# The w2 loads of the expert stages move from the sync engine's queue to ScalarE's

## Chip, cores and metric

One core of one Trainium2 chip. The metric is the device time of one execution in microseconds (us); the median of the runs counts. All arithmetic is in 32-bit floats.

## What is computed

256 tokens of width 1024 pass through two layers of a first block and one of a second. Each of the three has a mixer (attention, and in two of them a gated linear recurrence beside it) and then a mixture of 32 experts. What bears on this case is the mixture:

```python
xr = xt[tok]
return (jax.nn.silu(xr @ w1[e]) * (xr @ w3[e])) @ w2[e]
```

w1 and w3 of an expert are 1024 x 512, w2 is 512 x 1024: 2 MB each (2,097,152 bytes), 6 MB for an expert, 32 experts in each of the three stages. Each token goes to two experts. The kernel reads the weights of every expert, whichever tokens it has. In the second block the three matrices are called w_gate, w_up and w_down.

## The kernel before, in words

The program runs mixer, experts, mixer, experts, mixer, experts. The expert stage is one function, `expert_stage` (from L151), built three times. It sorts the tokens by expert, so that each expert has a window of 32 seats in each of two tiles, and then runs one round over the 32 experts (further rounds run only if an expert has more tokens than seats).

**Buffers.** w1, w3 and w2 have three slots each (`Experts`, L75). Expert e uses slot e mod 3 for w3 and w2. The w1 of expert 3 goes to spare places in x and h, so that later w1 sit one slot lower and are asked for one expert earlier. The first three experts are asked for before the loop, in the mixer or in the stage's head.

**TensorE** (`tensor`, `step` at L427) does for expert e, in this order: `up_first(e)` (w1, L348), `turn(e-1)` (two transposes, L371), `up_second(e)` (w3, L348), `scatter(e-2)` (L406), `turn_sel` for every second expert (L395), `down(e-1)` (w2, L385). It says on semaphores what it has finished: `w1_used`, `up_done`, `down_done`. After expert 30's `up_second` the order is written out (L454 to L470): `down(29)`, `turn(30)`, two scatters, `turn_sel`, `down(30)`, `up_first(31)`, `up_second(31)`, scatter, `turn(31)`, `down(31)`, scatter. The last w3 and the last w2 are loaded in halves, each with its own semaphore (L118, L123).

**The sync engine (SP)** asks for all weights (`sync`, L218). In the loop its order for each step is: w3 of expert off once `up_done` says that the slot's last user is through, w2 of expert off-1 once `down_done` says so, w1 of expert off+1 once `w1_used` says so (`refill`, L248). At the end: w3(30), w2(29), w2(30), w1(31), w3(31) in halves, w2(31) in halves (L264 to L272). After the loop it asks for the next mixer's first three blocks, as `w1_used`, `up_done` and `down_done` reach their last values (L281 to L284).

**ScalarE** (`scalar`, L501) does for each expert `hidden(e)` (silu of the w1 product, L573), `window(u, e+2)` (two copies that cut the columns of expert e+2, L564), and in the third stage alone `result(e-1)`: it waits for `down_done` and copies half of the output (L479). In the first two stages VectorE takes the whole output with its gate (L482). VectorE does the rest: the product with w3's output, the copies of the transposes (L836, L839).

Of the kernel before, what the change touches and what calls it, by code (L numbers as in the profile page):

```python
# [16 lines left out]
E = 32  # L17
# [23 lines left out]
class Stage:  # L41
# [7 lines left out]
    def sem(self, name):  # L49
        self.sems.append(self.nc.alloc_semaphore(name=f"{self.name}_{name}"))  # L50
        return self.sems[-1]
# [99 lines left out]
def expert_stage(nc, stage, experts, x, h, hT, gate1, scale2, shift2, gate2, norm_w, consts, mem, ps, x_banks, turn_banks, following=None, store=None,  # L151
# [32 lines left out]
    down_done, dve_step = sem("down"), sem("dve_step")  # L184
# [23 lines left out]
    PAIRS = E // 2  # L208

    def steps(eng):  # L210

        return eng.value_load(nsteps[0:1, 0:1], min_val=1, max_val=ROUNDS)
# [5 lines left out]
    def sync(sp, loads=None):  # L218

        sp.wait_ge(out_made, 4)  # L220
        experts.load_up(sp, 2, 0, 1)
        sp.wait_ge(x_kept, 4)
        experts.load_down(sp, 2, 0, 1)
        sp.wait_ge(rows_ready, TILES)
        sp.wait_ge(placed, 1)
        experts.load_spare(sp, 0, x)
        sp.wait_ge(steps_ready, 1)
        sp.wait_ge(gathered, len(GATHERS))
        experts.load_spare(sp, 1, h)
        rounds = steps(sp)  # L230
        with sp.Fori(0, rounds) as r:
            def refill_w1(k, off):

                early = isinstance(k, int) and k == 0 and off <= experts.SPARE + 3
                sp.wait_ge(w1_used, r * E + k * 6 + (off - 3 if early else off - 2))
                experts.load_w1_of(sp, (off - 1) % 3, k * 6 + off)

            def refill_w3(k, off):

                sp.wait_ge(up_done, r * E + k * 6 + (off - 2))  # L240
                experts.load_w3_of(sp, off % 3, k * 6 + off)

            def refill_down(k, off):

                sp.wait_ge(down_done, r * E + k * 6 + (off - 2))
                experts.load_down_of(sp, off % 3, k * 6 + off)

            def refill(k, off):  # L248

                early = isinstance(k, int) and k == 0  # L250
                if early:
                    refill_w1(k, off + 1)
                refill_w3(k, off)
                if not early or off > 3:
                    refill_down(k, off - 1)
                if not early:
                    refill_w1(k, off + 1)

            for off in range(3, 6):
                refill(0, off)  # L260
            with sp.Fori(1, E // 6) as k:
                for off in range(6):
                    refill(k, off)
            last = E // 6  # L264
            refill_w3(last, 0)
            refill_down(last, -1)
            refill_down(last, 0)
            refill_w1(last, 1)
            sp.wait_ge(up_done, r * E + (E - 3))
            experts.load_last_w3(sp, 1)  # L270
            sp.wait_ge(down_done, r * E + (E - 3))
            experts.load_last_down(sp, 1)  # L272
            with sp.If(rounds > r + 1):

                sp.wait_ge(down_done, r * E + E)
                experts.load_spare(sp, 0, x)
                experts.load_spare(sp, 1, h)
                for slot, u, pair in ((0, 0, 0), (1, 1, 0), (2, 0, 1)):
                    experts.load_up(sp, slot, u, pair)
                    experts.load_down(sp, slot, u, pair)  # L280
        if following is not None:  # L281
            for n, freed in zip(range(following.AHEAD), (w1_used, up_done, down_done)):
                sp.wait_ge(freed, rounds * E)
                following.load(sp, n)  # L284
        if store is not None:
            sp.wait_ge(xw_ready, rounds * E + 1)
            loads(sp)
            for t in range(TILES):
                for c in range(2):
                    cols = slice(c * 512, (c + 1) * 512)  # L290
                    sp.wait_ge(end_ready, 2 * t + c + 1)
                    sp.dma_start(store[:, t, cols], h[:, t, cols]).then_inc(stored, 16)
            sp.wait_ge(stored, 16 * 2 * TILES)
# [183 lines left out]
    def copy_y(eng_copy, u, half):  # L477
        rows = slice(64 * half, 64 * half + 64)
        return eng_copy(y[rows, u, :], bank_Y[rows, :])  # L479
# [21 lines left out]
    def scalar(act):  # L501
# [58 lines left out]
        def window(u, at):  # L560

            for t in range(TILES):
                start = act.value_load(starts[0:1, t, bass.ds(at, 1)], min_val=0, max_val=PICKS)
                m = nc.scalar.copy(xw[:, u, :, t * SEATS:(t + 1) * SEATS], sorted_x[:, :, t, bass.ds(start, SEATS)])  # L564
            m.then_inc(xw_ready, 1)

        with act.Fori(0, rounds) as r:
            def hidden(e, u, first=False):

                act.wait_ge(up_done, e + 1)  # L570
                if not first:
                    act.wait_ge(hm_ready, e)
                nc.scalar.activation(sil, H1[u], ACT.Silu).then_inc(silu_done, 1)  # L573

            def result(e, u):

                if gate2 is None:
                    act.wait_ge(down_done, e + 1)
                    copy_y(nc.scalar.copy, u, 0).then_inc(y_copied[0], 1)

            window(1, r * E + 1)
            hidden(r * E, 0, True)
            hidden(r * E + 1, 1)
            result(r * E, 0)
            for u in range(2):
                window(u, r * E + (2 + u))
            with act.Fori(1, PAIRS - 1) as i:
                for u in range(2):
                    e = r * E + i * 2 + u
                    hidden(e, u)  # L590
                    window(u, e + 2)
                    result(e - 1, 1 - u)
            hidden(r * E + (E - 2), 0)
            result(r * E + (E - 3), 1)
            result(r * E + (E - 2), 0)
            hidden(r * E + (E - 1), 1)
            window(0, r * E + E)
            result(r * E + (E - 1), 1)
# [287 lines left out]
    def under_way(pool):  # L886
# [3 lines left out]
        for signal in (down_done, silu_done, hT_copied):  # L890
            pool.wait_ge(signal, 1)

    return sync, tensor, scalar, vector, out_made, under_way


# [3435 lines left out]
```

## Time and profile before

| | |
|---|---|
| median of 3 runs | 2014.52 us (2011.88 to 2015.36) |
| the profiled execution's own time | 2012.33 us |
| its span | 2010.6 us |
| TensorE busy | 1878.9 us (93%), mean granted clock 0.993 |
| ScalarE busy | 361.8 us (18%) |
| VectorE busy | 502.9 us (25%) |
| moved by DMA | 727.07 MB, mean 362 GB/s |
| DMA queue q1 | 725.26 MB |
| DMA queue q10 | 0.78 MB |

The span is the time from the first instruction to the last. The page cuts it into 40 slices of about 50 us; a "GB/s" figure stands for each. Engines are named PE (TensorE matmul), PEld (its weight load), DVE (VectorE), ACT (ScalarE), SP (the sync engine); a q behind a name (SPq, ACTq) marks what the engine's sequencer does, such as the issue of a DMA. A TensorE row says "busy" while the matmuls of a group run, whatever the pace at which their data came. All w1, w3 and w2 of the first two stages are called in_moe_w_dram in the rows; in the third they are in_w_gate_dram, in_w_up_dram and in_w_down_dram.

### The profile page before, as it was taken

The numbers are of one execution on the slowest core, as the hardware profiler recorded it, in microseconds if no ns is written. First come the engines' busy times: TensorE is split into PE (matmuls) and PEld (weight loads), VectorE is DVE, ScalarE is ACT, GpSimd is POOL, SyncE is SP. The second block draws the span as 40 slices with busy tenths as digits, with TensorE's granted clock in tenths as the row PEclk, the third lists the DMA queues.
The fourth block names the chain that finished last, engine by engine and source line by source line (L and its number), as shares of the span: only waits on it lengthen the run. The fifth ranks groups of instructions, "written<-read, shape, count | busy, mean of one in ns | idle before, by whom it ended". The sixth has DMA issues, their size and how long they took to land. (4 is left out here: it accounts for less than half of the span.)

```text
span 2010.6 us, 29251 instructions
## 1 busy us (share of the span) xinstructions
PE 1878.9 (93%) x11670; PEld 938.8 (47%) x11670; DVE 502.9 (25%) x1201; ACT 361.8 (18%) x804; POOL 3.1 (0%) x7
## 2 busy tenths in 40 slices
PE   6999999998888999999998888999999999998887
PEld 3444544444444345544444444455545544444443
DVE  1345311111111333511111111324544211111112
ACT  2332200000000232310000000224322111111111
POOL 0000000000000000000000000000000000000000
PEclk9999999999999899999999999999999999999999
DMA  9979999999999885899999999842238999999997
GB/s 355 313 264 349 423 426 426 427 428 428 428 428 416 297 288 197 355 427 426 427 428 428 428 428 427 284 156 96 85 126 342 419 426 427 427 428 428 428 428 304
DMA packets 117842, 727.07 MB, mean 362 GB/s; under 512 B 19471, under 2 KB 25978, under 8 KB 79754
## 3 DMA queue, kind: packets, MB, share of 16 engines
q1 hardware_dynamic: 116472, 725.26, 88.9%
q10 hardware_dynamic: 1298, 0.78, 0.2%
q8 instruction: 54, 0.88, 0.2%
q14 instruction: 18, 0.15, 0.0%
HBM read 724.17 MB, written 1.84 MB: 361 GB/s over the span
## 5 line engine op out<-in xcount | busy, mean ns | idle before, releaser
L348 PE MATMUL psum<-arena,norm_w 128*64 128x256 f32 x6048 | 722.4, 390 | 73.8 <-DMA arena<-in_moe_w_dram 46.7
L348 PEld LDWEIGHTS psum<-arena,norm_w 128*64 128x64 f32 x6048 | 419.9, 134 | 374.5 <-DMA arena<-in_moe_w_dram 68.2
L385 PE MATMUL psum<-arena,hT 128*64 128x512 f32 x1536 | 350.8, 598 | 6.4 <-DMA arena<-in_moe_w_dram 2.4
L573 ACT ACTIVATE hT<-psum 128x256 f32<-128x256 f32 x96 | 36.9, 384 | 994.8 <-PE psum L348 994.8
L385 PEld LDWEIGHTS psum<-arena,hT 128*64 128x64 f32 x1536 | 105.4, 136 | 210.3 <-issue 205.5
L2462 PE MATMUL psum<-arena,hT 128*128 128x512 f32 (+1 forms) x352 | 152.5, 582 | 0.4 <-DVE hT L2822 0.4
L482 DVE TENSOR_TENSOR hT<-psum,arena 128x512 f32<-128x512 f32 x64 | 44.3, 692 | 332.5 <-PE psum L385 332.5
L836 DVE COPY hT<-psum 128x256 f32<-128x256 f32 x96 | 40.8, 425 | 327.4 <-PE psum L371 327.4
L406 PE MATMUL psum<-hT 32*128 32x512 f32 x768 | 108.6, 638 | 2.4 <-DVE hT L482 1.6
L2462 PEld LDWEIGHTS psum<-arena,hT 128*128 128x128 f32 x352 | 64.3, 190 | 67.0 <-issue 63.9
L564 ACT COPY norm_w<-arena 128x256 f32 x192 | 78.7, 410 | 69.7 <-issue 69.5
L3817 PE MATMUL psum<-arena,hT 128*128 128x512 f32 x192 | 86.5, 605 | 0.9 <-DVE hT L4141 0.9
L839 DVE COPY hT<-psum 128x256 f32<-128x256 f32 x48 | 20.4, 425 | 231.2 <-PE psum L395 231.2
L3219 PE MATMUL psum<-arena,hT 128*128 128x512 f32 (+1 forms) x160 | 66.1, 568 | 1.6 <-PEq L1105 1.6
L479 DVE COPY hT<-psum 64x512 f32<-64x512 f32 x32 | 22.2, 695 | 166.1 <-PE psum L385 166.1
L3817 PEld LDWEIGHTS psum<-arena,hT 128*128 128x128 f32 x192 | 36.3, 194 | 46.3 <-issue 46.3
L371 PE MATMUL psum<-const_ident,hT 128*128 128x128 f32 x192 | 48.5, 334 | 3.5 <-DVE hT L834 3.5
L371 PEld LDWEIGHTS psum<-const_ident,hT 128*128 128x128 f32 x192 | 30.3, 207 | 44.8 <-issue 36.5
L406 PEld LDWEIGHTS psum<-hT 32*128 32x128 f32 x768 | 30.3, 183 | 42.0 <-issue 36.6
L757 DVE TENSOR_SCALAR arena<-const_iota,arena 128x64 f32<-128x64 f32 x204 | 49.7, 309 | 0.1
L834 DVE TENSOR_TENSOR hT<-hT,psum 128x256 f32<-128x256 f32 x96 | 39.8, 415 | 32.9 <-ACT hT L573 32.0
L3219 PEld LDWEIGHTS psum<-arena,hT 128*128 128x128 f32 x160 | 30.3, 193 | 32.6 <-issue 31.2
(438 smaller groups left out, 1200.4 us busy)
## 6 DMA issues: line engine op xcount, KB each, us to landing
arena<-in_moe_w_dram SPq DMA_DIRECT2D x186, 2048.0 KB, 32.3
arena<-in_w_gate_dram SPq DMA_DIRECT2D x31, 2048.0 KB, 30.1
arena<-in_w_up_dram SPq DMA_DIRECT2D x31, 2048.0 KB, 28.7
arena<-in_w_down_dram SPq DMA_DIRECT2D x31, 2048.0 KB, 30.5
arena<-in_ada_w_dram SPq DMA_DIRECT2D x24, 2048.0 KB, 15.3
arena<-in_w_in_dram SPq DMA_DIRECT2D x10, 2048.0 KB, 8.5
arena<-in_odd_w_in_dram SPq DMA_DIRECT2D x6, 2048.0 KB, 10.8
arena<-in_even_w_in_dram SPq DMA_DIRECT2D x4, 2048.0 KB, 18.9
```

The lines of the kernel that those rows point to most:

```text
L348: m = nc.tensor.matmul(out[64 * half:64 * half + 64, :].rearrange("p (q c) -> p q c", c=2), xw[:, u, c, :], w[c].rearrange("p (q half c) - ...
L371: m = nc.tensor.transpose(HT[:, c, :], hm[:, c::2], ident[:, :])
L385: m = nc.tensor.matmul(bank_Y[64 * half:64 * half + 64, :], hTs[:, k % 2, (k // 2) * 64:(k // 2) * 64 + 64], experts.slots[slot][2][:, k, ...
L406: nc.tensor.matmul(bank_acc[2 * t + half][:, :], selT[rows, u, :], y[rows, u, :], start=False, stop=False, skip_group_check=True).then_inc ...
L482: return nc.vector.tensor_tensor(y[:, u, :], bank_Y, gate2[:, 0:512], ALU.mult)
L564: m = nc.scalar.copy(xw[:, u, :, t * SEATS:(t + 1) * SEATS], sorted_x[:, :, t, bass.ds(start, SEATS)])
L757: m = nc.vector.tensor_scalar(at, iota[:, 0:SEATS].unsqueeze(1).to_broadcast([P, 2, SEATS]), slots[:, t, bass.ds(g, 1)], comb[:, t, bass.d ...
L834: nc.vector.tensor_tensor(hm, sil, H3[u], ALU.mult).then_inc(hm_ready, 1)
L836: nc.vector.tensor_copy(hTs, HT).then_inc(hT_copied, 1)
L2462: m = nc.tensor.matmul(banks[t][:, 0:width], hT[:, k, t * P:(t + 1) * P], ring.tile(n, DC, width)[:, k, :], start=(k == 0), stop=(k == DC ...
L3219: m = nc.tensor.matmul(side_bank("P", n, t)[:, 0:width], hT[:, k, t * P:(t + 1) * P], blocks.tile(("P", n))[:, k, :], start=(k == 0), stop ...
L3817: m = nc.tensor.matmul(side_bank("P", n, t), hT[:, c, t * P:(t + 1) * P], ring.tile(n, DC, 512)[:, c, :], start=(c == 0), stop=(c == DC - 1))
```

## The change

The three w2 requests of the sync engine's loop are taken out. ScalarE makes them, with the same semaphore and the same value to wait for, behind `hidden`, `window` and `result` of the same step. Its loop over pairs of experts becomes one over groups of six, since the slot (e mod 3) and the column buffer (e mod 2) have to be constants in the text. The first three w2 are still asked for by SP, and so are all further rounds' first three.

```diff
@@ sync
-            def refill_down(k, off):
-
-                sp.wait_ge(down_done, r * E + k * 6 + (off - 2))
-                experts.load_down_of(sp, off % 3, k * 6 + off)
-
             def refill(k, off):
                 early = isinstance(k, int) and k == 0
                 if early:
                     refill_w1(k, off + 1)
                 refill_w3(k, off)
-                if not early or off > 3:
-                    refill_down(k, off - 1)
                 if not early:
                     refill_w1(k, off + 1)
...
             refill_w3(last, 0)
-            refill_down(last, -1)
-            refill_down(last, 0)
             refill_w1(last, 1)
             sp.wait_ge(up_done, r * E + (E - 3))
             experts.load_last_w3(sp, 1)
-            sp.wait_ge(down_done, r * E + (E - 3))
-            experts.load_last_down(sp, 1)
@@ scalar
+            def refill_down(k, off):
+
+                act.wait_ge(down_done, r * E + k * 6 + (off - 2))
+                experts.load_down_of(act, off % 3, k * 6 + off)
+
+            def act_step(k, off):
+
+                e, u = r * E + (k * 6 + off), off % 2
+                hidden(e, u)
+                window(u, e + 2)
+                result(e - 1, 1 - u)
+                refill_down(k, off + 2)
+
             window(1, r * E + 1)
             hidden(r * E, 0, True)
             hidden(r * E + 1, 1)
             result(r * E, 0)
             for u in range(2):
                 window(u, r * E + (2 + u))
-            with act.Fori(1, PAIRS - 1) as i:
-                for u in range(2):
-                    e = r * E + i * 2 + u
-                    hidden(e, u)
-                    window(u, e + 2)
-                    result(e - 1, 1 - u)
+            refill_down(0, 3)
+            for off in range(2, 6):
+                act_step(0, off)
+            with act.Fori(1, E // 6 - 1) as k:
+                for off in range(6):
+                    act_step(k, off)
+            for off in range(5):
+                act_step(E // 6 - 1, off)
+            e = r * E + (E - 3)
+            hidden(e, 1)
+            window(1, e + 2)
+            result(e - 1, 0)
+            act.wait_ge(down_done, r * E + (E - 3))
+            experts.load_last_down(act, 1)
             hidden(r * E + (E - 2), 0)
```

## Rows read from the trace of the kernel before

**Rows 1.** The page: TensorE's busy time, and the rate of all DMA by slice.

```profile
PE 1878.9 (93%) x11670; PEld 938.8 (47%) x11670; DVE 502.9 (25%) x1201; ACT 361.8 (18%) x804; POOL 3.1 (0%) x7
...
GB/s 355 313 264 349 423 426 426 427 428 428 428 428 416 297 288 197 355 427 426 427 428 428 428 428 427 284 156 96 85 126 342 419 426 427 427 428 428 428 428 304
```

**Rows 2.** Busy time by stretch: length, engines (instructions), PE clock, DMA share, GB/s.

```profile
406.00:600.00 194.00, 173.37 (x1214) 83.40 (x1212) 27.97 (x74) 16.82 (x42) 0.00 (x0) 1.00 1.01 428
...
1574.00:1755.00 181.00, 179.07 (x1288) 88.45 (x1286) 31.22 (x78) 25.80 (x58) 0.00 (x0) 1.00 1.01 427
1755.00:1970.00 215.00, 193.90 (x1364) 94.16 (x1362) 33.64 (x85) 26.77 (x60) 0.00 (x0) 1.00 1.01 428
```

**Rows 3.** Waits, 406 to 640 us, TensorE: total us, times, longest us.

```profile
PE psum L348 <- DMA arena<-in_moe_w_dram: 23.6, 28, 1.2
PE psum L385 <- DMA arena<-in_moe_w_dram: 1.1, 1, 1.1
```

**Rows 4.** Tile view, one w2 load of the third stage: issue, and its landing.

```profile
L129 SPq DMA_DIRECT2D arena<-in_w_down_dram x1: 333/333/333, 1905.1 to 1905.1; - x1
...
DMA to landing us min/median/max: 40.1/40.1/40.1
```

**Rows 5.** DMA view: packets by size, and issues with the median us to landing.

```profile
DMA packets 117842, 727.07 MB, mean 362 GB/s; under 512 B 19471, under 2 KB 25978, under 8 KB 79754
...
arena<-in_moe_w_dram SPq DMA_DIRECT2D x186, 2048.0 KB, 32.3
```

**Rows 6.** Timeline of TensorE, end of the third expert stage: start us, us, instruction.

```profile
1955.03 3.85 PE L348 MATMUL psum<-arena,norm_w 128*64 128x256 f32 x32 [0.62 <-DMA arena<-in_w_up_dram]
...
1960.25 3.65 PE L385 MATMUL psum<-arena,hT 128*64 128x512 f32 x16
...
1969.73 3.85 PE L348 MATMUL psum<-arena,norm_w 128*64 128x256 f32 x32 [0.60 <-DMA arena<-in_w_up_dram]
1974.73 3.65 PE L385 MATMUL psum<-arena,hT 128*64 128x512 f32 x16 [1.15 <-DMA arena<-in_w_down_dram]
...
1982.36 3.65 PE L385 MATMUL psum<-arena,hT 128*64 128x512 f32 x16
1985.85 7.42 PE L348 MATMUL psum<-arena,norm_w 128*64 128x256 f32 x64
```

**Rows 7.** Timeline of TensorE and SP around the end of the first stage.

```profile
621.72 3.84 PE L348 MATMUL psum<-arena,norm_w 128*64 128x256 f32 x32 [0.62 <-DMA arena<-in_moe_w_dram]
626.71 3.65 PE L385 MATMUL psum<-arena,hT 128*64 128x512 f32 x16 [1.15 <-DMA arena<-in_moe_w_dram]
...
641.53 17.99 SPq L2276 DMA_DIRECT2D arena<-in_odd_w_in_dram  x3
...
661.88 3.75 PE L3817 MATMUL psum<-arena,hT 128*128 128x512 f32 x4 [0.92 <-DVE hT L4141]
```

**Rows 8.** Tile view, the last w2 halves of the first stage: issues, and their landings.

```profile
L126 SPq DMA_DIRECT2D arena<-in_moe_w_dram x2: 328/380/432, 615.9 to 616.3; - x2
...
DMA to landing us min/median/max: 29.0/30.1/31.2
```

**Rows 9.** Timeline of ScalarE: one silu of the third stage, and its longest DMA issue.

```profile
36.45 0.82 ACTq L1277 DMA_DIRECT2D skew_scratch<-arena  x1
...
1944.22 0.38 ACT L573 ACTIVATE hT<-psum 128x256 f32<-128x256 f32 x1 [9.11 <-PE psum L348]
```

**Rows 10.** Timeline of the program's first 15 us, both queues in use.

```profile
1.19 0.68 SPq L1114 DMA_DIRECT2D arena<-in_ada_w_dram  x1
1.91 0.64 SPq L1118 DMA_DIRECT2D x<-in_x_dram  x1
...
2.82 0.31 ACTq L1229 DMA_DIRECT2D arena<-const_hot_causal_dram  x1
...
9.96 0.16 DVE L1202 COPY arena<-arena 33x8 f32<-33x8 f32 x1 [4.97 <-DMA arena<-const_hot_causal_dram]
...
11.88 3.64 PE L1136 MATMUL psum<-arena 128*32 128x512 f32 x16 [11.88 <-DMA arena<-in_ada_w_dram]
...
14.35 1.06 ACT L1251 ACTIVATE h<-x 128x1024 f32<-128x1024 f32 x1 [8.39 <-DMA x<-in_x_dram]
```

## The prediction

> **What bounds the kernel now.** I read the page first. TensorE is busy for 93% of the span, which looks like the bound, but the rate of all DMA stands at 426 to 428 GB/s in 22 of the 40 slices, and it falls only in the mixers [rows 1]. A plateau that flat is a limit. The busy time by stretch says which of the two holds where [rows 2]: from 1574 to 1755 us TensorE is busy for 179 of 181 us and the DMA engines are full as well; from 1755 to 1970 us TensorE is busy for 194 of 215 us at an unchanged 428 GB/s. So each expert stage begins with TensorE as the pace and a stock of loaded experts, the stock melts, and then the bytes set the pace. The first stage has the same second part (173 of 194 us). The waits tell what is late there: TensorE waits 28 times for a w1 or w3, at most 1.2 us each, and once for a w2 [rows 3]. With one queue and requests in the order of need, everything lands just before its use: a w2 asked for at 1905.1 us lands 40.1 us later [rows 4], and the median over 186 loads of the first two stages is 32.3 us [rows 5]. Those 40 us aren't transfer time but some eight loads standing in line.
>
> The timeline of TensorE at the end of the third stage shows the beat [rows 6]: `up_second` of experts 29 and 30 start at 1955.03 and 1969.73 us, 14.70 us apart, for three loads of 2.097 MB, so 4.90 us a load, which is 428 GB/s. Then comes the place on which I rest the forecast. `up_second(30)` waits for its w3 (1969.73), `down(29)` waits 1.15 us for its w2 (1974.73), and from there on TensorE waits for no DMA: `down(30)` at 1982.36 and expert 31 from 1985.85 run on data that are already there. Behind w3(30) TensorE has a fixed run of work, from 1969.73 to the end of the kernel, and **the landing of w3(30) starts it**. The five loads behind it in the line (w2(29), w2(30), w1(31), w3(31), w2(31)) take 5 x 4.90 = 24.5 us and land beside that work. The first stage has the same picture and the same 1.15 us wait [rows 7], with its last halves of w2 asked for at 616.3 and landing up to 31.2 us later, at 647.5 us [rows 8]. The second stage repeats it.
>
> **The change, part by part.** *Number and times of the requests.* 29 w2 of each stage, one of them in two halves, change queue. Nothing is asked for earlier: TensorE finishes `up_second(e)`, `down(e-1)`, `up_first(e+1)` in just the order in which SP asks for w3, w2, w1, so SP's wait for `down_done` never held a w1 back. Both engines wait for the same semaphore values. Cost 0, gain 0. The bytes are the same, and the DMA engines are full from the stage's head to its last load, so the moment at which the last byte lands doesn't move; I call it Z.
>
> *ScalarE's time.* An issue of such a load takes SP 0.33 us [rows 4]; the longest that ScalarE shows for any DMA is 0.82 us [rows 9]. 30 issues in a stage cost it 10 to 25 us of work. New is a wait for `down_done` in the first two stages (in the third `result` has it already). What is queued behind that wait is `hidden(e+1)`, and this needs `up_done` of e+1, which TensorE gives only after `down(e-1)` and then two passes of 3.85 us [rows 6], `up_first(e+1)` and `up_second(e+1)`: 7.7 us later at least. `window(e+2)` stands before the wait. ScalarE stands idle for 9.11 us before a silu [rows 9]; so the wait and the issue are covered, cost 0. If an issue blocked for over 7.7 us this cover would be gone; that is a rival below.
>
> *SP* loses 30 issues and their waits in a stage; what was queued behind them came later anyway. The branches of ScalarE's longer loop body are covered by the same 9 us. Cost 0.
>
> *The order in which the bytes land.* This is the term that counts. w2 is a third of the bytes. On its own queue a w2 no longer stands behind the w1 and w3 asked for before it. Does the second queue really overtake? One place of this trace has both in use [rows 10]: SP asks for 2 MB at 1.19 us and for x, 1 MB, at 1.91 us; ScalarE asks for a 49.5 KB table at 2.82 us, after both. VectorE uses the table at 9.96 us, TensorE the first 2 MB at 11.88 us, ScalarE x at 14.35 us. The later request on the other queue was ahead of both. So queues aren't drained in order of request. The Trainium skill (DMA: Bandwidth & Descriptors, Queues, rings and completion order) gives a rule that speaks against this change: each DMA engine goes round between the queues that have work, a packet of each. By that rule the split is one to one here and the result is the forecast's; by strict order of arrival it would be no change.
>
> How the engines are shared no row shows, so I bound it: ScalarE's queue gets between a third of the rate (its part of the bytes) and all of it while it has work. I take one half: there are two queues with work, and the packets of w1, w3 and w2 are alike in size (the 279 whole loads of the loops would be 128 packets each at 16 KB, 35,712, and the page leaves 38,088 packets of 8 KB or more) [rows 5].
>
> *Where the lead comes from.* With a half, a w2 needs 9.8 us from request to landing instead of 40.1 and then lies in its slot for some 30 us. Two more w2 lie there loaded than before, at an unchanged total, so w1 and w3 are about two loads behind, and TensorE, which now waits for these alone, is some 10 us behind its old place by the stage's late part. In the middle of a stage that lag grows in the place of waits and costs nothing by itself. It is paid at the end, where the run of work behind w3(30) starts later against a fixed Z.
>
> *The sum for one stage.* Count from the landing of w3(29), time 0. w3(30) lands one beat later, at 14.7. `down(28)` ends 8.9 us after `up_second(29)` starts (1955.03 to 1963.9) [rows 6], and then w2(31) is asked for. Of its 4.90 us of transfer a half share has done (14.7 - 8.9) / 2 = 2.9 by 14.7, so 2.0 are left, with w1(31) and w3(31), 9.8. w3(30) thus lands 11.8 us before Z instead of 24.5, which is 12.7 us later. Back come the 1.15 us that `down(29)` waited, since w2(29) is long there. Net **11.55 us a stage**. Is another load late instead? w1(31) and w3(31) have landed 11.8 us after w3(30), and `up_first(31)` starts 16.1 us after `up_second(30)` (15 without the wait). So no.
>
> With a third, 1.9 are done, 3.0 left, and the net is 24.5 - 12.8 - 1.15 = 10.6 us; with all of the rate w2(31) is through, and the net is 24.5 - 9.8 - 1.15 = 13.6 us.
>
> *Does a stage hand its delay on?* The next mixer's first blocks are asked for when `w1_used` is complete (641.53 us), and TensorE begins on them at 661.88, held by VectorE and not by a load [rows 7]. Both come from TensorE's progress, so they move together, and the queue is emptier. All of it is handed on: 3 x 11.55 = 34.7 us. Against the profiled execution's 2012.33 us this gives 2047.0 us. The median of the runs is 2.2 us above that execution; I state 2047 and keep the 2.2 for the range.
>
> **The rivals.**
>
> *No overtaking (no change).* The loads land in the order of need as before, since the small table of rows 10 is a poor stand-in for 2 MB loads. Time 2012 to 2015 us. Against it stands that the table did pass 3 MB. Chance 0.11.
>
> *Half-way.* w2 overtakes by one load only, because a queue already eight loads deep keeps the engines longer than its turn. Then w3(30) lands about 4.90 us later: 3 x 4.9 = 15, or 2027 us. Chance 0.10.
>
> *A fuller pipe (faster).* Two queues keep the 16 engines better supplied, at the plateaus, and the rate rises. For: no row shows what sets the plateau at 428. Against: the engines' share reads 1.00 or 1.01 there, so there is nothing to fill [rows 2]. The three stages move 3 x 29 x 6.29 = 547 MB in 1278 us at 428; to pay for 34.7 us the rate would have to pass 440 GB/s, which no slice shows. At 445 it gains 49 us against the 35: 1998 us. Chance 0.05.
>
> *ScalarE is held by its issues (much slower).* If an issue blocks until the queue has room, silu is late. At 9.8 us blocked against 7.7 us of cover, TensorE loses 2.1 us for each of some 14 experts a stage that it paces itself (181 us [rows 2], at 194 / 215 of a beat of 14.7 us, is 13.3 us each): 3 x 14 x 2.1 = 88 us on top, 2135 us. Against: one w2 is in the queue at a time, where SP kept eight loads in line at 0.33 us an issue [rows 4]. Chance 0.04.
>
> **How the numbers follow.** The forecast's own case has 0.70: 3 x 10.6 to 3 x 13.6 is 32 to 41 us, the plateaus' spread (426 to 428 GB/s) is worth 3 us each way on 1278 us, and the median lies 2.2 us above, so 2041 to 2058. The range takes in the half-way case: 2026 to 2059, leaving out 0.20 (no overtaking 0.11, fuller pipe 0.05, held ScalarE 0.04). A measurement of this kernel can tell about 0.2%, 4 us, from no change. Slower by more: 0.70 + 0.10 + 0.04 = 0.84. Within it: 0.11. Faster: 0.05.
>
> **What would show it.** The DMA view should list w2 on ScalarE's queue, landing after some 10 us, and SP's loads in over 40 us in the late part. Late in a stage TensorE should wait for w3 once a beat, about 2 us, and for w2 never; `down(29)` should follow `up_second(30)` at once. The last load to land should be w3(31), about 12 us after `up_second(30)` starts, at about the old Z. Plateaus should stay at 428, silus should start as soon as `up_second` ends, and the gap between the last load of a stage and the next mixer's first should open. The forecast is wrong if w2 still takes 30 to 40 us, if the plateau moves, or if a mixer swallows the delay.

## The result, and the profile after

The changed kernel takes 2042.42 us (median of 4 runs, 2040.16 to 2047.06) against 2014.94 us for the kernel before: 1.0142 times, 95% interval 1.013 to 1.0155, so 26 to 31 us slower. The forecast was 2047 us in a range of 2026 to 2059. The profiled execution took 2043.87 us, 31.5 us above the profiled one of before (forecast on that footing: 34.7 us).

The page of the changed kernel, to be read against [rows 1] and [rows 5]: busy times, rate by slice, the two queues, and the issues with their median us to landing.

```profile
PE 1892.9 (93%) x11670; PEld 946.7 (46%) x11670; DVE 502.4 (25%) x1201; ACT 361.4 (18%) x804; POOL 3.1 (0%) x7
...
GB/s 362 297 267 352 427 426 425 428 427 427 428 427 342 288 289 200 346 427 426 428 427 428 427 428 425 220 153 95 83 124 367 412 427 426 428 427 427 427 428 222
...
q1 hardware_dynamic: 103512, 542.80, 66.4%
q10 hardware_dynamic: 14258, 183.24, 21.3%
...
arena<-in_moe_w_dram SPq DMA_DIRECT2D x130, 2048.0 KB, 37.7
arena<-in_moe_w_dram ACTq DMA_DIRECT2D x56, 2048.0 KB, 14.0
```

The plateaus stand where they stood, at 425 to 428 GB/s. 183 MB have moved to q10. In the first two stages a w2 now lands 14.0 us (median) after it is asked for, and the w1 and w3 need 37.7 us; before, the median over all three was 32.3 us. ScalarE's busy time is the same to 0.4 us. So the bytes came at the same rate in another order.

The end of the first stage on TensorE, to be read against [rows 7]; start us, us, instruction, and in brackets the idle time before it.

```profile
603.55 3.84 PE L337 MATMUL psum<-arena,norm_w 128*64 128x256 f32 x32 [0.56 <-DMA arena<-in_moe_w_dram]
...
619.50 5.16 PE L337 MATMUL psum<-arena,norm_w 128*64 128x256 f32 x32 [2.46 <-DMA arena<-in_moe_w_dram]
...
633.68 3.84 PE L337 MATMUL psum<-arena,norm_w 128*64 128x256 f32 x32
637.36 3.60 PE L374 MATMUL psum<-arena,hT 128*64 128x512 f32 x16
...
648.29 7.42 PE L337 MATMUL psum<-arena,norm_w 128*64 128x256 f32 x64
...
672.48 8.04 PE L3827 MATMUL psum<-arena,hT 128*128 128x512 f32 x13 [0.92 <-DVE hT L4151]
```

(L337 is L348 of before, L374 is L385.) `up_second(29)` starts at 619.50, after a wait of 2.46 us for its w3. In this stage `up_second(30)` starts at 633.68 without any wait, and `down(29)` at once behind it, at 637.36 instead of 626.71: 10.65 us late. `up_first(31)` starts at 648.29 and the next mixer's L3827 at 672.48 instead of 661.88, which is 10.60 us late: the mixer has swallowed nothing.

The last loads of that stage in the changed kernel, by the tile view: issues, and below each its landings. They answer to [rows 8].

```profile
L121 SPq DMA_DIRECT2D arena<-in_moe_w_dram x2: 327/376/426, 607.4 to 607.8; - x2
...
DMA to landing us min/median/max: 36.6/38.0/39.4
```

```profile
L126 ACTq DMA_DIRECT2D arena<-in_moe_w_dram x2: 334/396/457, 629.7 to 630.1; - x2
...
DMA to landing us min/median/max: 10.6/12.9/15.2
```

The halves of w3(31), asked for 22 us ahead of those of w2(31), land after them: 607.8 + 39.4 = 647.2 us against 630.1 + 15.2 = 645.3. The last landing, Z of the prediction, was at 647.5 before. It hasn't moved. In the second stage it went from 1272.0 to 1282.8 us, by the 10.6 us that the first stage had handed on and 0.2.

In the other two stages `up_first(31)` starts, before and after, at 1261.76 and 1283.06, and at 1985.85 and 2017.38 us. The whole is late by 10.6, 21.3 and 31.5 us after the first, second and third stage, so **10.6, 10.7 and 10.2 us a stage**. That is one execution: another of the same kernel (`changed_again` below) reads 7.8, 11.2 and 9.1, so a single stage's figure is good to some 2 or 3 us. The changed kernel's rows of stages two and three, `up_second(30)` and then `up_first(31)`:

```profile
1268.45 3.84 PE L337 MATMUL psum<-arena,norm_w 128*64 128x256 f32 x32 [1.50 <-DMA arena<-in_moe_w_dram]
...
1283.06 7.42 PE L337 MATMUL psum<-arena,norm_w 128*64 128x256 f32 x64
...
2002.63 3.84 PE L337 MATMUL psum<-arena,norm_w 128*64 128x256 f32 x32 [1.23 <-DMA arena<-in_w_up_dram]
...
2017.38 7.42 PE L337 MATMUL psum<-arena,norm_w 128*64 128x256 f32 x64
```

Here, other than in the first stage, `up_second(30)` does wait for its w3, 1.50 and 1.23 us.

TensorE's waits from 406 to 640 us, against [rows 3]:

```profile
PE psum L337 <- DMA arena<-in_moe_w_dram: 24.0, 15, 3.0
```

The total is that of before (24.0 against 24.7 us with the one for w2), but in 15 waits instead of 29, with a longest of 3.0 instead of 1.2 us, and none for w2. TensorE's lag began earlier: from 256 to 406 us it was busy for 150.0 of 150 us before and is busy for 143.3 now. By `up_second(28)` it is 11.3 us behind (603.55 against 592.29). Whether such a lag costs anything is decided at the stage's end, as the runs below show.

### The profile page after: what moved, and what is told of

Its sections match the earlier page's. It is cut to its first block and busy times, and to the rows that moved or that the text cites. A ratio compares the mean times of both kernels' runs of the same rounds, so it can differ in the third digit from the quotient of the medians.

```text
span 2042.1 us, 29232 instructions
## 1 busy us (share of the span) xinstructions
PE 1892.9 (93%) x11670; PEld 946.7 (46%) x11670; DVE 502.4 (25%) x1201; ACT 361.4 (18%) x804; POOL 3.1 (0%) x7
## 3 DMA queue, kind: packets, MB, share of 16 engines
q10 hardware_dynamic: 14258, 183.24, 21.3%
## 5 line engine op out<-in xcount | busy, mean ns | idle before, releaser
L337 PE MATMUL psum<-arena,norm_w 128*64 128x256 f32 x6048 | 743.8, 398 | 92.5 <-DMA arena<-in_moe_w_dram 59.1
L337 PEld LDWEIGHTS psum<-arena,norm_w 128*64 128x64 f32 x6048 | 431.9, 138 | 398.8 <-DMA arena<-in_moe_w_dram 73.4
L374 PE MATMUL psum<-arena,hT 128*64 128x512 f32 x1536 | 350.6, 598 | 1.8 <-DVE hT L846 1.8
L374 PEld LDWEIGHTS psum<-arena,hT 128*64 128x64 f32 x1536 | 102.3, 136 | 207.0 <-issue 206.4
L3827 PE MATMUL psum<-arena,hT 128*128 128x512 f32 x192 | 86.9, 607 | 0.9 <-DVE hT L4151 0.9
L3827 PEld LDWEIGHTS psum<-arena,hT 128*128 128x128 f32 x192 | 36.4, 195 | 46.6 <-issue 46.6
## 6 DMA issues: line engine op xcount, KB each, us to landing
arena<-in_moe_w_dram SPq DMA_DIRECT2D x130, 2048.0 KB, 37.7
arena<-in_ada_w_dram SPq DMA_DIRECT2D x24, 2048.0 KB, 15.2
```

The costliest lines, as they stand in the source:

```text
L337: m = nc.tensor.matmul(out[64 * half:64 * half + 64, :].rearrange("p (q c) -> p q c", c=2), xw[:, u, c, :], w[c].rearrange("p (q half c) - ...
L374: m = nc.tensor.matmul(bank_Y[64 * half:64 * half + 64, :], hTs[:, k % 2, (k // 2) * 64:(k // 2) * 64 + 64], experts.slots[slot][2][:, k, ...
L3827: m = nc.tensor.matmul(side_bank("P", n, t), hT[:, c, t * P:(t + 1) * P], ring.tile(n, DC, 512)[:, c, :], start=(c == 0), stop=(c == DC - 1))
```

## Experiments

Each ratio is to the kernel before, run on the same chip, with its 95% interval; it is estimated from all runs of both, and so isn't quite the quotient of the medians. "w2 on SP" means in its old place in SP's order.

### ScalarE's program without its loads

```diff
             def refill_down(k, off):
 
                 act.wait_ge(down_done, r * E + k * 6 + (off - 2))
-                experts.load_down_of(act, off % 3, k * 6 + off)
```

This is the changed kernel's ScalarE (loop of six, waits) over the SP of before.

> ScalarE has the changed kernel's loop over six experts and its waits for down_done, but asks for nothing; all w2 stay on SP as before. Theory 'order' (w2 on a queue of its own overtakes, w1 and w3 land later, paid behind w3(30) at the end of each stage): nothing changes, 2015 us, within 4. Rival 'ScalarE' (its new waits and longer loop body delay silu and columns): most of the 27 us stay, 2035 to 2042. Rivals 'clock' (TensorE's granted clock falls more often because its waits are longer) and 'two queues' (the second queue costs something for each load): 2015 as well.

2015.05 us, 1.0004 (0.9995 to 1.0013). The waits and the longer loop cost nothing. Of the rival "ScalarE" only the issues are left, which this run doesn't have. They are 0.33 us each, and in the changed kernel ScalarE still stands idle before a silu, as the row from its timeline shows:

```profile
607.45 0.38 ACT L562 ACTIVATE hT<-psum 128x256 f32<-128x256 f32 x1 [11.34 <-PE psum L337]
```

### w2 on ScalarE's queue for a part of the stage

Two kernels cut the stage at expert 26. One leaves the loads up to 25 on ScalarE's queue, the other the loads from 26 on.

```diff
@@ early_w2: ScalarE below 26, SP from 26
+                if isinstance(k, int) and k * 6 + off - 1 >= 26:
+                    refill_down(k, off - 1)
...
+                if not isinstance(k, int) or k * 6 + off + 2 < 26:
+                    refill_down(k, off + 2)
```

> w2 of experts 3 to 25 of each stage on ScalarE's queue, w2 of 26 to 31 on SP's as before. 'Order': the lag of w1 and w3 in mid-stage is there, but behind w3(30) stand five loads again, so nothing is paid: 2015 us, up to 2020. 'Two queues' (a cost for each load on the second queue): 23 of 29 loads, so 4/5 of 27 us, about 2036. 'Clock': the falls in mid-stage stay, about 13 of them at 1.3 us of TensorE's time each: 2027 to 2032.

2013.62 us, 1.0006 (0.9997 to 1.0015). With 23 of 29 w2 on the second queue nothing is lost, though the mean granted clock of the profiled execution is 0.985 as against 0.993. "Two queues" falls, and so does "clock" as the cause of the whole; what a fall on a stage's last passes adds is worked out further down.

```diff
@@ late_w2: SP below 26, ScalarE from 26
+                if (not early or off > 3) and (not isinstance(k, int) or k * 6 + off - 1 < 26):
+                    refill_down(k, off - 1)
...
+                if isinstance(k, int) and k * 6 + off + 2 >= 26:
+                    refill_down(k, off + 2)
```

> w2 of experts 3 to 25 on SP's queue as before, w2 of 26 to 31 alone on ScalarE's. 'Order': the full price, since only what stands behind w3(30) counts: 2038 to 2043 us. 'Two queues': 6 of 29 loads, about 2021. 'Clock': few falls, 2018 to 2022.

2043.24 us, 1.0143 (1.0127 to 1.0158): the full price from the last six loads alone. So the price is one of the stage's end, and six experts are enough to bring it about.

### How many of the last w2 go back to SP

The changed kernel with the last 3 (then 2, 4, 5) w2 of a stage asked for by SP and no longer by ScalarE. SP's part for three:

```diff
             refill_w3(last, 0)
+            refill_down(last, -1)
+            refill_down(last, 0)
             refill_w1(last, 1)
             sp.wait_ge(up_done, r * E + (E - 3))
             experts.load_last_w3(sp, 1)
+            sp.wait_ge(down_done, r * E + (E - 3))
+            experts.load_last_down(sp, 1)
```

> As the changed kernel, but w2 of experts 29, 30 and 31 are asked for by SP in their old places. 'Order': behind w3(30) stand w2(29), w2(30), w1(31), w3(31), w2(31), five loads as before: 2015 us, up to 2019. 'Two queues': 26 of 29 loads, about 2039. 'Clock': 2030 to 2040.

2026.0 us, 1.0061 (1.0047 to 1.0075). A miss: the order behind w3(30) is that of before, and 12 us are still lost, 4.1 a stage. Its TensorE, first stage, shows why. From its timeline:

```profile
588.08 3.84 PE L346 MATMUL psum<-arena,norm_w 128*64 128x256 f32 x32 [2.98 <-DMA arena<-in_moe_w_dram]
593.29 3.65 PE L383 MATMUL psum<-arena,hT 128*64 128x512 f32 x16
...
605.79 3.65 PE L383 MATMUL psum<-arena,hT 128*64 128x512 f32 x16
...
618.65 3.65 PE L383 MATMUL psum<-arena,hT 128*64 128x512 f32 x16
...
629.98 3.60 PE L383 MATMUL psum<-arena,hT 128*64 128x512 f32 x16
```

The last wait for a load ends at 588.08. After it `down` follows `down` at 12.5 and 12.9 us, TensorE's own pace, where the line of loads needs 14.70 us a beat. The loads are on time again: w3(30), asked for at 592.0, lands 28.6 us later, at 620.6. TensorE isn't: at 588.08 it is 10.5 us behind its old place (577.59), and it can make up about 2 us a beat. `down(29)` starts at 629.98, still 3.3 us behind the 626.71 of before. This gave the theory "lag": a stage pays what is left of TensorE's lag when it has worked off about 1.85 us in each beat since its last wait for a load. Three runs test it.

> As the changed kernel, but w2 of 30 and 31 asked for by SP. The run before this one (last three on SP, 2026.0 us, 4.0 us a stage) showed that the price isn't only what stands behind w3(30). Theory 'lag': by mid-stage TensorE is some 10 us behind, and once SP has all loads it makes up only what its own pace allows, 14.7 - 12.85 = 1.85 us a beat. One expert fewer on SP: 4.0 + 1.85 = 5.85 us a stage, 2031 to 2033 us. Rival 'order' as predicted (four loads behind w3(30), 24.5 - 19.6 - 1.15 = 3.75 us a stage): 2025 to 2027.

2035.04 us, 1.011 (1.0094 to 1.0125), 7.4 us a stage by the ratio. That is above what both had said, and far from the 2025 to 2027 of "order".

> As the changed kernel, but w2 of 28 to 31 asked for by SP. 'Lag': one beat more of recovery, 4.0 - 1.85 = 2.15 us a stage: 2019 to 2022 us. 'Order': five loads behind w3(30), nothing left to pay: 2014 to 2016.

2021.71 us, 1.0038 (1.0024 to 1.0052), 2.6 us a stage: as "lag" had it.

> As the changed kernel, but w2 of 27 to 31 asked for by SP. 'Lag': between last4_sp (1.0038 of before) and early_w2 (six on SP, 1.0006): 2.5 - 1.85 = 0.7 us a stage, 2015 to 2018 us. 'Order' as predicted: 2014, as with any number from three up.

2017.42 us, 1.0012 (1.0002 to 1.0023), 0.8 us a stage: as "lag" had it; "order" had no loss, 0.0002 outside the interval, so this run alone wouldn't decide.

The start of the x64 group of expert 31 in the third stage gives the same order in one execution each: 1985.85 us before [rows 6]; 1985.07, 1990.56, 1995.23, 1999.52, 2005.90 with six, five, four, three and two on SP; 2017.38 with none. Single stages scatter more: with three on SP they lost 3.2, 3.8 and 6.7 us in this order.

| w2 on SP at the stage's end | 6 | 5 | 4 | 3 | 2 | none |
|---|---|---|---|---|---|---|
| ratio to before | 1.0006 | 1.0012 | 1.0038 | 1.0061 | 1.011 | 1.0142 |

### w3 instead of w2

w3 goes to ScalarE behind the silu, w2 back to SP.

```diff
+            def refill_w3(k, off):
+
+                act.wait_ge(up_done, r * E + k * 6 + (off - 2))
+                experts.load_w3_of(act, off % 3, k * 6 + off)
+
+            def act_step(k, off):
+
+                e, u = r * E + (k * 6 + off), off % 2
+                hidden(e, u)
+                refill_w3(k, off + 3)
+                window(u, e + 2)
+                result(e - 1, 1 - u)
```

> w3 on ScalarE's queue behind the silu, w2 back on SP's. 'Lag': w3 now overtakes, w1 and w2 are two loads behind, TensorE some 10 us, and only the last one or two beats run without waits, so 7 to 10 us a stage: 2036 to 2045 us. 'Order' as predicted: w2(29) has three loads behind it instead of four, 4.9 us a stage: 2028 to 2031. Rival 'w2 alone is special' (its wait on down_done in ScalarE's stream): near 2015.

2036.75 us, 1.0116 (1.0101 to 1.0132), 7.7 us a stage. So the loss isn't peculiar to w2: w3 on a queue of its own makes the others late too (w1 wasn't tried). The price is in the range of "lag". TensorE waits here for w1 (L339, the third stage's in_w_gate_dram) as it waited for w3 there:

```profile
PE psum L339 <- DMA arena<-in_w_gate_dram: 24.4, 13, 3.5
```

### The same queue, asked later

w2 of expert e+1 is asked for right behind the silu of e.

```diff
                 hidden(e, u)
+                refill_down(k, off + 1)
                 window(u, e + 2)
                 result(e - 1, 1 - u)
-                refill_down(k, off + 2)
```

> w2 stays on ScalarE's queue, but that of expert e+1 is asked for right behind the silu of e, some 10 us later than in the changed kernel, so that it lies loaded and unused for about 10 us less, 0.7 of a load of 4.9 us. 'Lag': TensorE is 3.3 us less behind, 10.5 - 3.3 = 7 us a stage, 2033 to 2038 us. If what matters is only that the queues are two, and not how early w2 lands: as the changed kernel, 2040 to 2044.

2044.41 us, 1.0154 (1.0141 to 1.0168): a miss, no better than the change. From its timeline, first stage:

```profile
631.24 3.86 PE L337 MATMUL psum<-arena,norm_w 128*64 128x256 f32 x32 [2.15 <-DMA arena<-in_moe_w_dram]
634.92 3.61 PE L374 MATMUL psum<-arena,hT 128*64 128x512 f32 x16
```

w3(30) is what TensorE waits for, and `down(29)` is 634.92 - 626.71 = 8.2 us late, against 10.65 in the profiled execution of the changed kernel. That looked like the gain hoped for, but it shows none: in the changed kernel's other execution (`changed_again`) the same start is at 634.53, 7.8 us late. The second stage lost 7.7 us, the third 13.1. The windows of its trace near that stage's head show a rate that the changed kernel hasn't:

```profile
1605.00:1650.00 45.00, 45.00 (x326) 22.15 (x326) 7.64 (x20) 6.55 (x15) 0.00 (x0) 1.00 0.97 397
```

The same window of the changed kernel:

```profile
1605.00:1650.00 45.00, 43.17 (x316) 21.98 (x318) 7.41 (x17) 7.50 (x17) 0.00 (x0) 1.00 1.00 425
```

28 GB/s less for 45 us are 1.3 MB, 3 us of transfer by estimate, which would come back at the end as a later Z. In the third stage `up_second(30)` also took 5.44 instead of 3.84 us, partly on the lower clock, but so it did in the second, which lost only 7.7. So the 3 us are a guess at the cause, and two more runs test it: the changed kernel again, and the later request from expert 13 on alone.

> The changed kernel itself, beside the next two on the same chip: 2040 to 2045 us by every theory; it is there to compare w2_later_mid with.

2041.13 us, 1.0134 (1.0119 to 1.0148).

In the other run `act_step` gets two more arguments: the third asks for the next w2 right behind the silu, the fourth leaves out one request where the two ways meet.

```diff
+            for off in range(6):
+                act_step(1, off, False, off == 5)
+            with act.Fori(2, E // 6 - 1) as k:
+                for off in range(6):
+                    act_step(k, off, True)
```

> As w2_later, but the later request only from expert 13 on; up to expert 12 w2 is asked for as in the changed kernel. w2_later came out at 2044 us, not at 2033 to 2038: its profile shows the first stage 8.2 us late at down(29), as worked out, but the third 13.1 us, with DMA at 295 to 401 GB/s for some 25 us near that stage's head, where nothing was asked for. Theory 'lag, and DMA kept full': with the head as in the changed kernel only the gain is left, 8.2 to 9 us a stage: 2036 to 2041 us, below the changed kernel of this call by 2 to 6 us. Rival 'the time of the request doesn't matter': equal to the changed kernel within 2 us.

2037.19 us, 1.0109 (1.0094 to 1.0123), 3.9 us below the changed kernel beside it. The four runs of each don't overlap (at most 2038.8 against at least 2039.66), but the intervals of the two ratios do, so a gain from the later request is likely and small. The window near the head reads 425 GB/s again, and against the 1.0154 of w2 asked late throughout the difference is clear: while the stock is small it pays to ask early.

## Why the prediction was right

**Requests, issues and ScalarE's waits at cost 0**: right. The run without the loads measured 1.0004.

**Z doesn't move**: right, 647.2 against 647.5 us in the first stage, at unchanged plateaus. (In `changed_again` it is at 645.0.)

**w2 overtakes**: right. The halves of w2(31) passed those of w3(31). That excludes the rival "no overtaking", which would have given 2012 to 2015 us, and with it a queue served in order of request. The share of one half was assumed for a transfer of 9.8 us; a load takes 14.0 us from issue to landing. Short of the transfer there is a fixed part: loads of 2 MB on a queue that isn't backed up, the mixers' in_w_in_dram, have a median of 8.2 us here and 8.5 us before, where the bytes need 4.90, so some 3.5 us. What is left, 10.5 us, is close to a half share. The Trainium skill (DMA: Bandwidth & Descriptors, Queues, rings and completion order) has the engines go round between queues by packet. With packets of like size that would be an even split, and the trace agrees with it roughly (10.5 against 9.8 us). The share was never measured by itself.

**The price of one stage**: 11.55 us forecast, 10.2 to 10.7 measured in one execution and 7.8 to 11.2 in another. The forecast had w3(30) land 12.7 us later; it landed 10.6, 12.1 and 11.6 us later in the three stages. Two terms of that were mis-sized, and in part they cancel, so that the sum came this close is partly luck. The distance from w3(30) to Z before the change was put at five loads, 24.5 us; the rows themselves give 647.5 - 621.7 = 25.8. And w2(31) was to have 2.9 of its 4.90 us done when w3(30) lands, which left 11.8 us behind it; the runs show 14.9, 14.4 and 14.3 us from that landing to Z, three whole loads. In the second and third stage w2(31) was asked for 8.9 us after `up_second(29)` begins, as forecast; most likely its first bytes come only after a fixed part of the kind just named, so that nearly all of it stood behind w3(30), but no row times them. A third, smaller term wasn't in the sum: in the first stage `up_second(29)` took 5.16 instead of 3.84 us on the lower clock.

**The landing of w3(30) starts the last run of work**: right for this kernel, with an exception. In the second and third stage, and in the first of `changed_again` (1.18 us), `up_second(30)` waits for its w3. In the first stage w3(30), asked for at 594.0, landed 38.4 us later, at 632.4, and TensorE came 1.3 us after it, just what the slow `up_second(29)` had cost. The second and third stage of `changed_again` are alike: w3(30) lands 1.3 and 1.0 us before TensorE comes, behind an `up_second(29)` of 5.18 and 5.45 us. So up to about 1.3 us of a stage's price is the clock's.

**What the prediction lacked** is that this landing is only one of two things that can start it; the other is TensorE's own lag. Putting back the last loads alone showed it: with three on SP w3(30) lands early enough, and TensorE comes 5.7 us after it (626.30 against 620.6). The lag can be worked off only by the difference of two paces: 14.70 us a beat for the bytes and some 12.7 for TensorE. By the ratios a stage loses 0.8, 2.6, 4.1 and 7.4 us with five, four, three and two on SP: steps of 1.8 and 1.5 us, near the 1.85 of "lag", and then one of 3.3 us. The traces suggest why that step is larger: with two on SP TensorE's last wait for a load is at `up_second(29)` in all three stages, which leaves one beat; with three it is at expert 27, 28 and 27, which leaves two or three. One expert more on SP thus gave up to two beats more, 1.85 to 3.7 us. Each is one execution and the ratios' intervals are 1 us a stage wide to either side, so this isn't shown.

**Handed on**: right. The mixers gave nothing back (10.60 us late at the next mixer's first matmul, 21.3 and 31.5 us at the ends of stages two and three).

**The rivals.** "Fuller pipe" is out: the rate stayed at 428 GB/s with both queues at work. "ScalarE is held" is out: its issues took 0.33 to 0.35 us from 406 to 612 us. "Half-way" is out for this kernel; its time, 2027 us, came up in the run with three loads on SP, by another way.

Of the signs named ahead, four were off in size. The waits for w3 came about every second beat at 2 to 3 us rather than at each beat at 2 us. The last load was w3(31), 13.5 us after `up_second(30)` starts in the first stage and 14.3 in the others (12 were named). A w2 took 14 us and not some 10. SP's loads were to need over 40 us in the late part; the last ones of the three stages took 34.9 to 40.5 us, where w3(30) had taken 40.2 before.

No kernel of this study beats the one before: the nearest, w2 on ScalarE up to expert 25, is level with it.

## What to carry to other kernels

Where one queue keeps the DMA engines full, as here, its order is the schedule: w2 or w3 on a queue of its own came sooner, and the loads that were needed next paid for it. Before splitting a stream that already fills the DMA engines over two queues, look at which load starts the compute engine's last run of work and at what stands behind that load; a lag taken up in the middle is free only if enough beats remain to work it off at the difference of the two paces. A later request may trim the overtaking a little, but while the stock is small it leaves the DMA engines short of work (397 against 425 GB/s in one window here).

## What was not expected of the hardware

TensorE's granted clock fell more often. By the windows of the changed kernel, against 1.00 in the first row of [rows 2]:

```profile
406.00:600.00 194.00, 174.12 (x1196) 85.85 (x1198) 28.53 (x76) 15.59 (x39) 0.00 (x0) 0.96 1.01 428
```

A pass of 32 matmuls takes 3.84 us at the 2.4 GHz level. In the expert stages of the changed kernel 14 such passes took 5.1 to 6.6 us; over the one at 619.50 the granted clock reads 0.72, so it stood at 1.2 GHz for a part of it. Every one of them, in all the runs of this study, came behind a wait of 1.75 us or more, and not every such wait was followed by a fall: in the changed kernel 11 weren't (nor was the one of 2.98 us at 588.08 in the run with three on SP). Before the change no pass was slow; its waits from 406 to 640 us were at most 1.2 us, and the clock stayed at 1.00 from 406 to 600. The L337 matmuls took 398 ns in the mean instead of 390. In a stage's middle this cost nothing, as the run with w2 on ScalarE up to expert 25 shows; on `up_second(29)` or `up_second(30)` it is time lost, up to 1.3 and 1.6 us.
